# Two issuers for the expert weights: odd loads from ScalarE, even loads from SyncE, and a down projection whose last chunk runs by groups

## The reference

```
logits = (xt @ w_router);  top_logit, top_idx = top_k(logits, 2);  gates = softmax(top_logit)
# tokens are sorted by expert into blocks; for each block xb of expert e:
hid = silu(xb @ w_gate[e]) * (xb @ w_up[e])        # w_gate, w_up: 8 x 1024 x 3584
yb  = hid @ w_down[e]                              # w_down: 8 x 3584 x 1024
y[token] += yb * gate                              # h + y is the output, 256 x 1024
```

## Time and profile before

| What | us |
|---|---|
| median of 3 runs | 1308.36 |
| the profiled execution, its device time | 1308.11 |
| its span, first to last instruction | 1306.3 |
| ahead of the first item | 446.6 |
| one item in steady state (1 to 5) | 105.63 |
| PE idle in the whole span | 25.1 |

### The profile page before, as it was taken

How to read it: one execution, slowest core, us unless ns; L and a number is a source line. 1 busy time by engine, 2 the same in 40 slices (tenths; PEclk the granted TensorE clock), 3 DMA queues, 4 the chain that set the end, 5 groups by cost and what they waited for, 6 DMA issues and landing times.

```text
span 1306.3 us, 36546 instructions
## 1 busy us (share of the span) xinstructions
PE 1281.2 (98%) x16212; PEld 812.1 (62%) x16212; DVE 673.2 (52%) x945; ACT 252.1 (19%) x386; POOL 49.7 (4%) x46
## 2 busy tenths in 40 slices
PE   9999999999899999999999999999999999999998
PEld 8998899988767654544653554554454465354344
DVE  5885555554885666155245425615705524542471
ACT  5564534442743200000000000000000000000000
POOL 1001000000000340000000000000000000000021
PEclk9999999999999899999999999999999999999999
DMA  9867555566523899999999999999999999999995
GB/s 321 271 209 232 174 183 192 186 221 195 197 98 130 346 402 409 415 419 417 417 418 417 418 418 418 419 416 420 417 416 419 414 417 418 395 420 417 417 406 223
DMA packets 114209, 442.67 MB, mean 339 GB/s; under 512 B 9284, under 2 KB 55700, under 8 KB 83348
## 3 DMA queue, kind: packets, MB, share of 16 engines
q1 hardware_dynamic: 107904, 424.75, 82.7%
q10 hardware_dynamic: 4820, 11.53, 2.6%
q0 software_dynamic: 1344, 4.20, 0.9%
HBM read 434.12 MB, written 12.08 MB: 342 GB/s over the span
## 4 chain that ended last, share of the span: by engine, by line
PE 84%; DMA 5%; SPq 4%; DVE 4%; ACT 2%; issue 1%; DVEq 0%; ACTq 0%
PE bank L2069 19%; PE bank L2118 19%; PE bank L2087 11%; PE bank L1619 8%; PE bank L1620 8%; PE bank L1621 8%; PE bank L2099 6%; SPq L544 2%; DMA raw<-in_moe_w_down 2%; DMA raw<-in_moe_w_up 2%; SPq L547 1%; DMA raw<-in_hgrn_w_in 1%; DVE w_lo L1009 1%; ACT w_hi L715 1%; PE bank L1866 1%
## 5 line engine op out<-in xcount | busy, mean ns | idle before, releaser
L1009 DVE TENSOR_TENSOR w_lo<-raw,w_hi 128x2048 fp32r<-128x2048 f32 x62 | 141.5, 2289 | 98.5 <-ACT w_hi L715 98.5
L2118 PE MATMUL bank<-more_ring,hidT 128*32 128x256 f32 x3072 | 168.7, 379 | 0.0
L2069 PE MATMUL bank<-more_ring,xT 128*32 128x512 f32 (+1 forms) x1632 | 160.0, 548 | 0.0
L1527 DVE TENSOR_TENSOR sums<-raw 128x1024 f32<-128x1024 f32 (+1 forms) x31 | 34.0, 1096 | 209.9 <-PE bank L2087 121.0
L2118 PEld LDWEIGHTS bank<-more_ring,hidT 128*32 128x32 f32 x3072 | 100.1, 110 | 65.7 <-issue 0.3
L1619 PE MATMUL bank<-ht_hi,w_hi 128*128 128x256 f32 x464 | 129.4, 279 | 1.6 <-DVE ht_lo L1023 1.5
L2069 PE MATMUL bank<-raw,xT 128*32 128x384 f32 (+1 forms) x1392 | 130.9, 530 | 0.0
L1620 PE MATMUL bank<-ht_lo,w_hi 128*128 128x256 f32 x464 | 128.9, 278 | 0.0
L1621 PE MATMUL bank<-ht_hi,w_lo 128*128 128x256 f32 x464 | 128.9, 278 | 0.0
L2118 PE MATMUL bank<-raw,hidT 128*32 128x256 f32 x2304 | 126.1, 379 | 0.5 <-DMA raw<-in_moe_w_down 0.5
L715 ACT ACTIVATE w_hi<-raw 128x2048 fp32r<-128x2048 f32 x62 | 118.6, 1918 | 38.1 <-PE bank L1621 37.7
(11 more groups left out here) (342 smaller groups left out, 1729.0 us busy)
## 6 DMA issues: line engine op xcount, KB each, us to landing
more_ring<-in_moe_w_down SPq DMA_DIRECT2D x64, 1024.0 KB, 20.0
raw<-in_moe_w_down SPq DMA_DIRECT2D x48, 1024.0 KB, 19.6
more_ring<-in_moe_w_gate SPq DMA_DIRECT2D x40, 1024.0 KB, 19.9
more_ring<-in_moe_w_up SPq DMA_DIRECT2D x40, 1024.0 KB, 20.2
raw<-in_moe_w_gate SPq DMA_DIRECT2D x34, 768.0 KB, 16.3
more_ring<-in_moe_w_up SPq DMA_DIRECT2D x32, 768.0 KB, 18.8
raw<-in_moe_w_gate SPq DMA_DIRECT2D x24, 1024.0 KB, 19.5
raw<-in_moe_w_up SPq DMA_DIRECT2D x24, 1024.0 KB
```

Of the source, the lines that this page charges most:

```text
L1009: nc.vector.tensor_tensor(w_lo[:, slot, :], raw[:, slot_raw, :], plain(w_hi[:, slot, :]), SUB).then_inc(split_ready, 1)
L1527: nc.vector.tensor_tensor(t1, b12, b11, SUB).then_inc(sum_ready[0], 1)
L2069: ins = nc.tensor.matmul(out_banks[j][GTOK * c:GTOK * c + GTOK, 0:w], xT[:, j, kt, :], chunk[:, c], start=kt == 0, stop=kt == KT - 1)
L2118: ins = nc.tensor.matmul(banks[1 + j // 2][GTOK * c:GTOK * c + GTOK, 256 * (j % 2):256 * (j % 2) + 256], hidT[sup][:, g, m, :], ring_place ...
```

## The change

- SP's loop over the items 1 and up issues only the even loads. The odd ones are issued by ACT on its own queue: loads that wait for up_used in `loads_of_item`, between ACT's silus and copies of the same item; loads 1 to 17 of the next item, which wait for dn_used, in `loads_of_next`, during the down projection. The loads of item 0 all stay with SP. `load_rows` stays with SP.
- ACT's loop is written as item 0, a loop, and the last item, since the first issues no odd loads of its own and the last none of a next one.
- The last down chunk runs by groups of columns instead of by half, so that bank 1 is complete two steps of four matmuls before the end; PE signals it with dn_front, and ACT's copies wait for that instead of dn_used.
- At the end PE multiplies the left half of the columns first, as soon as ACT has copied it (yb_front), and the right half when all of yb is there. DVE's adds and SP's stores follow that order.
- POOL fetches the second choices after load 43 instead of 44 (`third_last`). DVE's copies of bank 2 move out of `one_item` into `copy_results`, at the start of the next item; after the last item they come behind the two adds of the second choices.

```diff
-                for k in range(N_UP):
+                for k in range(0, N_UP, 2):
                     wait_used(n, k)
                     load(e, k)
                 sp.wait_ge(x_ready, n + GRPS)
                 sp.sem_inc(sp_pace, 1)
                 load_rows(n + 1)
-                for k in range(N_UP, N_LOADS):
+                for k in range(N_UP, N_LOADS, 2):
...
-            last_but_one = N_LOADS - 2
+            third_last = N_LOADS - 3
...
+            def load_odd(e, k):
+
+                act.sem_inc(act_pace, 1)
+                if k < N_UP:
+                    act.dma_start(ring_place(k), up_source(e, k)).then_inc(load_full[k % SIGNALS], 16)
+                else:
+                    act.dma_start(ring_place(k).rearrange("p (k c) -> p k c", k=2), down_source(e, k - N_UP)).then_inc(load_full[k % SIGNALS], 16)
...
+            def loads_of_item(n, e, above, to):
+
+                for k in range(1, N_LOADS, 2):
+                    m = overwritten(k)
+                    if m >= 0 and above < UP_USED[m] <= to:
+                        act.wait_ge(up_used, n * UP_STEPS + UP_USED[m])
+                        load_odd(e, k)
...
+                if following:
+                    loads_of_next(n, e_next, range(N_DN - 1))
+                act.wait_ge(dn_front, n + 1)
+                nc.scalar.activation(yb[:, 0:512], banks[1][0:CAP, :], ACT.Copy).then_inc(yb_front, 1)
...
+            copy_results(n_items)
             dve.wait_ge(early_added, 2 * TT)
...
+                steps = [(half, j) for half in range(2) for j in range(GRPS)]
+                if i == N_DN - 1:
+                    steps = [(half, j) for j in range(GRPS) for half in range(2)]
...
+            for half in range(2):
+                if half == 0:
+                    pe.wait_ge(yb_front, n_items)
+                else:
+                    pe.wait_ge(yb_ready, n_items * 2 + 1)
+                for t in range(TT):
```

More of the change, by code:

```diff
@@ L400, in build_program @@
         dn_used = sem("dn_used")
+        dn_front = sem("dn_front")
+        yb_front = sem("yb_front")
         gathered = sem("gathered")
@@ L604, in _ @@
                 load_rows(n + 1)
-                for k in range(N_UP, N_LOADS):
+                for k in range(N_UP, N_LOADS, 2):
                     wait_used(n, k)
                     load(e, k)
-            for t in range(TT):
-                for half in range(2):
+            for half in range(2):
+                for t in range(TT):
                     cut = slice(512 * half, 512 * half + 512)
-                    sp.wait_ge(combined, 2 * t + half + 1)
+                    sp.wait_ge(combined, 2 * half + t + 1)
                     sp.dma_start(out[0][P * t:P * t + P, cut], h[:, t, cut]).then_inc(stored, 16)
@@ L969, in _, with loads_of_next, one_item @@
             act.wait_ge(routed, 1)
-            n_items = act.value_load(items[0:1, 16:17], min_val=E, max_val=MAX_ITEMS)
-            with act.Fori(0, n_items) as n:
+            n_last = act.value_load(items[0:1, 17:18], min_val=E - 1, max_val=MAX_ITEMS - 1)
+            def load_odd(e, k):
[10 more added lines that the diff above has]
+                        load_odd(e, k)
+            def loads_of_next(n, e, chunks):
+                for k in range(1, N_LOADS, 2):
+                    m = overwritten(k)
+                    if m < 0 and m + N_LOADS - N_UP in chunks:
+                        act.wait_ge(dn_used, n * N_DN + (m + N_LOADS - N_UP + 1))
+                        load_odd(e, k)
+            def one_item(n, own=True, following=True):
+                if own:
+                    e = act.value_load(items[0:1, bass.ds(n, 1)], min_val=0, max_val=E - 1)
+                if following:
+                    e_next = act.value_load(items[0:1, bass.ds(n + 1, 1)], min_val=0, max_val=E - 1)
                 for sup, (_, w) in enumerate(SUPERS):
-                    act.wait_ge(up_used, n * UP_STEPS + PHASE_END[2 * sup])
+                    begin, mid, end = PHASE_END[2 * sup - 1] if sup else 0, PHASE_END[2 * sup], PHASE_END[2 * sup + 1]
+                    if own:
+                        loads_of_item(n, e, begin, mid - 1)
+                    act.wait_ge(up_used, n * UP_STEPS + mid)
                     if sup:
@@ L993, in _ @@
                 act.sem_inc(act_pace, 1)
+            one_item(0, own=False)
+            with act.Fori(1, n_last) as n:
+                one_item(n)
+            one_item(n_last, following=False)
         @block.vector
@@ L1597, in _ @@
             with dve.Fori(1, n_items) as n:
+                copy_results(n)
                 one_item(n, ring_place)
@@ L1604, in _ @@
                                                op0=MUL, op1=ADD).then_inc(early_added, 1)
+            copy_results(n_items)
             dve.wait_ge(early_added, 2 * TT)
-            for t in range(TT):
-                for half in range(2):
+            for half in range(2):
+                for t in range(TT):
                     part = h[:, t, 512 * half:512 * half + 512]
-                    dve.wait_ge(end_full, 2 * t + half + 1)
+                    dve.wait_ge(end_full, 2 * half + t + 1)
                     nc.vector.tensor_tensor(part, part, END_BANKS[2 * t + half][:, :], ADD).then_inc(combined, 1)
@@ L2110, in down_products @@
             def down_products(i):
-                for half in range(2):
+                steps = [(half, j) for half in range(2) for j in range(GRPS)]
+                if i == N_DN - 1:
+                    steps = [(half, j) for j in range(GRPS) for half in range(2)]
+                for half, j in steps:
                     q = 2 * i + half
                     sup, m = (0, q) if q < SUPERS[1][0] // P else (1, q - SUPERS[1][0] // P)
[L2115 to L2122, removed]
+                    for c in range(4):
+                        d, g = (j, c) if c < GRPS else (GRPS, j)
+                        ins = nc.tensor.matmul(banks[1 + j // 2][GTOK * c:GTOK * c + GTOK, 256 * (j % 2):256 * (j % 2) + 256],
+                                               hidT[sup][:, g, m, :],
+                                               ring_place(N_UP + i)[:, D * half + 256 * d:D * half + 256 * d + 256],
+                                               start=i + half == 0 and j != 1, stop=i == N_DN - 1 and half == 1,
+                                               skip_group_check=True)
+                    if i == N_DN - 1 and half == 1 and j == 1:
+                        ins.then_inc(dn_front, 1)
                 ins.then_inc(dn_used, 1)
@@ L2185, in _ @@
             pe.wait_ge(end_sel_ready, 1)
-            pe.wait_ge(yb_ready, n_items * 2 + 1)
-            for t in range(TT):
-                for half in range(2):
+            for half in range(2):
+                if half == 0:
+                    pe.wait_ge(yb_front, n_items)
+                else:
+                    pe.wait_ge(yb_ready, n_items * 2 + 1)
+                for t in range(TT):
                     nc.tensor.matmul(END_BANKS[2 * t + half][:, :], end_selT[:, P * t:P * t + P], yb[:, 512 * half:512 * half + 512],
```

16 lines of the change are left out of this document (11 added, 5 removed).

## The result

The changed kernel takes 1317.32 us, the median of 11 runs (1313.39 to 1322.31), against 1308.36 us (11 runs, 1305.66 to 1311.93) for the kernel before on the same chip. The ratio is 1.0062, with a 95% interval of 1.0048 to 1.0076. The profiled execution took 1315.91 us, its span is 1313.8 us.

What follows compares the result with a forecast made beforehand. DMA, needing some 109.1 us an item against PE's 105.63, sets the end once the ring's slack is spent. Stalls of +9.1 us less 1.4 at the end give +7.7 on 1308.4, about 1316 us; range 1301.5 to 1323.

Steps and rivals of the forecast that it cites:

- rival C: Level streams, but ACT held by its yb store delays silus: up to 11 us, 1308 to 1316 us; chance 0.06.
- The growth of 3.5 us an item: Down chunks' landing time in the kernel before: DMA falls 3.5 us further behind PE each item.
- Part 1, no gain in rate: Odd loads on ACT's queue: two weight queues raise DMA rate only +0.4%, costing +9.1 us; +11.5 at no gain.
- Part 1, packet by packet: DMA engines alternate queues per packet, so SP's 24 small row packets per engine stop even loads for 7.5 us.
- rival B: Faster: small rows do not hold up even loads and both streams stay level, 1304.6 us; chance 0.04.
- Part 1, the even loads carry the backlog: Even loads fall back 5.6 us an item against odd ones until PE stalls on them; stalls of 14.4 us.
- the ring: Weight buffer, a third of an item: hides landing times up to about 28.0 us before PE stalls.
- my formula: Backlog hidden with two queues: 28.0 / 2 + 2.5 = 16.5 us; stalls at no gain 33.3 - 16.5 = 16.8 us.
- Part 2: ACT's wait for its yb store, now behind one or two odd loads, lasts some 10 us and stays hidden.
- S: Yb store lands behind odd loads; its wait holds ACT, delaying silus and odd loads: hidden, or up to 11 us.
- U: Small token rows on SP's queue hold up the even loads, which fall back 5.6 us an item.
- Part 3: Kernel's end: earlier first copy lets PE go on right after the last down projection, saving 1.4 us.

Runs made afterwards that it cites:

- late_wait_split2: Changed kernel, but ACT awaits its yb store only before rewriting yb, and 128 of 384 token rows are fetched by ACT's queue: 1312.34 us, ratio 1.0032.
- late_wait: Changed kernel, but ACT waits for its store of yb only before it writes yb again: 1324.3 us, ratio 1.0098 to the kernel before.
- experiment 5: The run late_wait_split2: late_wait with 128 of 384 token rows fetched by ACT's queue, 256 by SP's; 1312.34 us, ratio 1.0032.
- 2: The run late_wait: changed kernel with ACT's wait for its yb store moved to just before yb is rewritten; 1324.3 us, ratio 1.0098.
- experiment 6: Changed kernel with 128 of 384 token rows fetched by ACT's queue, 256 by SP's, ACT still waiting right behind its yb store: 1322.18 us, ratio 1.0103.
- experiment 8: As late_wait_split2, but 160 token rows fetched by ACT's queue and 224 by SP's: 1316.5 us, ratio 1.0064 to the kernel before.

## Why the prediction was right in its time, and where it was not in its steps

The time came out; the mechanism did not. The stalls that the sum is made of, PE waiting for even loads, are absent from the changed kernel, and the sign that the prediction gave for rival C, PE's longest waits being for the silu, is what its trace shows. So the hit is luck in good part.

**What bounds the kernel**: right. The items stay at 105.63 us until a stall, and the DMA sets the end. The growth of 3.5 us an item is read from items 1 and 5 alone: in the kernel before the down chunks of item 6 take 26.7 us, so from item 1 to item 7 it is 3.0.

**Part 1, no gain in rate**: no slice is above 419 GB/s with two streams of weights, and items 1 to 4 of late_wait_split2 run at 417 to 418, as with one queue. The +0.4% that I took, from the gather and the store, was not there; the bound at no gain, +11.5, held. "DMA: Bandwidth & Descriptors" in the Trainium skill, Rules for kernel authors, says that spreading DMAs over queues brings no bandwidth; the rates here agree. The items lost 10.9 us more than before, which is near 11.5 but was not lost in that way.

**Part 1, packet by packet**: right. In the changed kernel all 384 small packets of item 1 run between 593.6 and 602.9 us, 9.3 us where I had 7.5. The queues in that window:

```profile
q10 hardware_dynamic: 403, 2.95, 76.9%
q1 hardware_dynamic: 461, 0.85, 24.3%
```

403 packets of ACT's queue pass beside 461 of SP's, with 3.5 times the bytes. Counts as near as these, and as in the earlier trace rows, would also fit twelve of one queue for twelve of the other. The start of the stretch tells them apart: from 593.8 to 594.8 us 44 packets of SP's queue run beside 47 of ACT's, while twelve small ones in a row on each of 16 engines would be up to 192. The Trainium skill's other rule, "DMA: Bandwidth & Descriptors", Queues, rings and completion order, has an engine drain typically 9 to 17 descriptors before it switches. It would give rival B, and these windows do not bear it out.

**Part 1, the even loads carry the backlog**: right as a mechanism (late_wait: 34.6 against 10.9 us), but in the changed kernel only up to item 3, where SP's chunks land in 24.6 us (25 was predicted). ACT's were to stay under 12 and are at 21.3. Alone, the mechanism costs about what I summed: 15.6 us of waits in late_wait against 16.8 at the rate found (14.4 at the +0.4%). The three chunks that PE waits for there land after 34.69, 37.07 and 38.37 us and it waits 3.17, 5.56 and 6.86 (length less busy time of the items): the ring hides 31.5 us of such a landing each time, where I had 28.0. Put into my formula, 31.5 / 2 + 2.5 = 18.3 and 33.3 - 18.3 = 15.0 us of stalls. What I had no term for is the slower clock behind each stall, 7.5 us more in the items. So late_wait loses 12.8 us by its ratio and 17.4 us between the spans, where I had summed 7.7.

**Part 2 is the step that failed**, the overlap that I took for given. "The store waits for one or two of them, some 10 us: hidden." It lands after 12.0 us in item 1, but 18.7 in item 3 and 26.5 in item 5. I took the odd loads as early whatever ACT does. But ACT issues them itself, so its wait delays them, and an odd load that is late also lands late: the state in which the wait is hidden does not last. That is rival C, to which I gave 0.06, and its sizes fit: waits of up to 4.0 us for the silu in three items (8.8 of the 11.3 us that PE waits in items 4 to 7), and late odd loads of w_up. Its premise of level streams does not: they start 7 us apart (19.1 and 12.0 in item 1). I had C and the forecast as alternatives. They are one system, and S works against U. With the small packets taken off SP's queue, the wait costs 8 to 10 us; with them on, it saves some 5.

**Part 3**: -1.4 us predicted, -1.5 in the traces. L2251 starts 0.05 us before the chain has the down projection end (PE's timeline of the changed kernel; the same rows show DVE's copies in time, at 1306.01):

```profile
1305.15 0.59 ACT L1028 ACTIVATE yb<-bank 96x512 f32<-96x512 f32 x1 [35.01 <-PE bank L2175]
...
1305.89 3.68 PE L2251 MATMUL bank<-yb,end_selT 96*128 96x512 f32 x8
1306.01 0.42 DVE L1645 COPY yb<-bank 96x256 f32<-96x256 f32 x1 [6.38 <-PE bank L2175]
```

**The sum**: 1316 predicted, 1317.3 measured. It is no proof of the steps: a gain that was not there (2.4 us), a clock that I had not reckoned with, and a wait that I called hidden and that took the place of the stalls came out nearly even. That is luck.

## What to carry to other kernels

When work for one consumer in a fixed order is dealt to two DMA queues, do not count on the queues staying level: count the packets of everything on each, not the bytes, because here 384 small packets on one queue let as many large ones of the other pass. The consumer then waits for the queue that is behind, and what the other has prefetched does not help it. No version with two queues here beat the one with a single queue in the consumer's order. An engine that issues loads should not wait for a DMA on the same queue, since that wait grows with the backlog (12 to 28 us here, against 7.9 on a queue of its own); but before such a wait is taken away, ask what it was holding back, since here it kept the down chunks of the queues within some 7 us of each other, and they lay 27 apart in item 5 without it.

## What the runs showed of the hardware that was not expected

A long wait of PE costs more than its length. The last stall of late_wait, in windows of 2 us (columns as above):

```profile
1268.00:1270.00 2.00, 1.54 (x32) 0.65 (x20) 0.40 (x1) 0.38 (x1) 0.00 (x0) 1.00 1.03 428
...
1272.00:1274.00 2.00, 0.00 (x0) 0.00 (x0) 2.00 (x6) 0.00 (x0) 0.00 (x0) 0.50 1.03 430
...
1280.00:1282.00 2.00, 2.00 (x27) 0.99 (x23) 0.00 (x0) 0.00 (x0) 2.00 (x2) 0.50 1.01 414
1282.00:1284.00 2.00, 2.00 (x44) 1.25 (x40) 0.00 (x0) 0.00 (x0) 2.00 (x1) 0.97 0.57 229
```

```profile
1276.40 10.77 PE L2180 MATMUL bank<-more_ring,hidT 128*32 128x256 f32 x144 [6.86 <-DMA more_ring<-in_moe_w_down]
```

PE stands still for 6.86 us, in which the granted clock falls from 1.00 to 0.50 (from 2.4 to 1.2 GHz), and it comes back only at about 1282 us, 5.6 us after PE has gone on. The 144 products take 10.77 us; at the 36.26 us for 672 of an undisturbed down projection they would take 7.77. So the stall of 6.9 us costs 9.9, nearly all of the 10.1 us by which the item is longer. In the changed kernel the clock falls in the same way behind the silu waits (0.98 over items 6 and 7): the 192 products behind them take 22.50 and 22.29 us, against 20.60 in the earlier trace rows. In the kernel before, the stall of 5.3 us is spread over many short waits, and the clock in item 7 stays at 1.00.

The drift between two queues is large for small causes. Eight small packets an engine and item, moved from one queue to the other, take the gap between the down chunks of item 5 from 26.6 to 4.9 us (experiment 5 against 2), and with the wait kept they turn which queue is late in items 2 and 3 (experiment 6 against the changed kernel). Two more packets turn it without the wait (experiment 8 against 5), by more than their count explains. In late_wait the lag shrank only in the items behind a stall of PE.
